# Moving matmul operands in on-chip memory: the distance from the streamed operand to the loaded one, modulo 128 words

## The reference, cut to what matters

```python
# block 1: norm, in-projection, gated-recurrence and window attention, out-projection,
#          memory cross-attention, then for each token 128 of 16384 experts:
u = expert_down[eidx]
a = gelu(einsum('thkd,td->thk', u, xb))
y = einsum('thkk,thkd->td', g * a, expert_up[eidx])       # h = h + y
...
# block 2, twice: a mixer and a feed-forward
h = h + mixer(rms_norm(h)) ; h = h + conv_ffn(rms_norm(h), w_up, w_down)
def conv_ffn(hn, w_up, conv_w, conv_b, w_down):
    u, v = split(hn @ w_up, 2)                            # 1024 -> 2 x 2816
    return (silu(depthwise_conv3(u)) * v) @ w_down        # 2816 -> 1024
```

## Time and profile before

| | |
|---|---|
| time, median of 3 runs | 1670.4 us (1668.63 to 1673.06) |
| profiled execution, first to last instruction | 1670.5 us |
| PE / PEld busy | 1652.9 / 1542.5 us |
| DVE / ACT busy | 1237.3 / 935.2 us |
| DMA | 323.40 MB, mean 194 GB/s |
| TensorE clock granted | full speed (2.4 GHz), shown as 1.00, in every stretch below (from 17 us on) |

### The profile page before, as it was taken

The page is one execution under the profiler, slowest core; times in us unless marked ns, Lnnn a source line. Parts: engine busy times, 40 slices in busy tenths (PEclk is TensorE's granted clock), DMA queues, the critical chain, the costliest instruction groups (busy, mean ns, idle before and its releaser), DMA issues.

```text
span 1670.5 us, 30280 instructions
## 1 busy us (share of the span) xinstructions
PE 1652.9 (99%) x12006; PEld 1542.5 (92%) x12006; DVE 1237.3 (74%) x1896; ACT 935.2 (56%) x1139; POOL 242.8 (15%) x333
## 2 busy tenths in 40 slices
PE   8999999999999999999999999999999999999999
PEld 8999999999999999988888888999999888899987
DVE  6875467999998666667676676887888565769974
ACT  7885565555546555545555454786545357565542
POOL 0000000004667676211010110000000000100000
PEclk9999999999999999999999999999999999999999
DMA  7445344776555555777777776533555544345553
GB/s 304 152 152 180 120 159 157 231 233 213 189 178 191 190 189 191 270 240 238 245 235 239 241 238 222 221 133 139 184 185 195 180 174 152 124 156 203 200 188 115
DMA packets 73804, 323.40 MB, mean 194 GB/s; under 512 B 8663, under 2 KB 9047, under 8 KB 55744
## 3 DMA queue, kind: packets, MB, share of 16 engines
q1 hardware_dynamic: 58736, 285.18, 50.1%
q0 software_dynamic: 5568, 19.38, 3.7%
q10 hardware_dynamic: 9360, 16.92, 2.7%
HBM read 303.62 MB, written 17.83 MB: 192 GB/s over the span
## 4 chain that ended last, share of the span: by engine, by line
PE 83%; DVE 12%; ACT 4%; issue 1%; DMA 0%; SPq 0%; ACTq 0%; DVEq 0%
PE bank L605 14%; PE bank L606 13%; PE bank L607 13%; PE bank L986 7%; PE bank L985 7%; PE bank L987 7%; PE bank L938 5%; PE bank L942 5%; PE bank L941 5%; DVE lo_u L2299 3%; PE bank L950 2%; DVE wlo L1914 2%; DVE oh L2310 1%; ACT whi L1350 1%; DVE pos L2196 1%
## 5 line engine op out<-in xcount | busy, mean ns | idle before, releaser
L1586 ACT ACTIVATE hi_u<-raw_u 128x1024 fp32r<-128x1024 f32 x256 | 271.8, 1062 | 279.6 <-PE bank L985 165.2
L1914 DVE TENSOR_TENSOR wlo<-raw,whi 128x2048 fp32r<-128x2048 f32 (+1 forms) x141 | 314.7, 2232 | 105.6 <-PE bank L605 83.3
L1350 ACT ACTIVATE whi<-raw 128x2048 fp32r<-128x2048 f32 x137 | 263.1, 1920 | 77.6 <-PE bank L605 74.7
L938 PE MATMUL bank<-xh,hi_u 128*128 128x256 f32 x1024 | 291.9, 285 | 1.5 <-DVE lo_u L2299 1.2
L2299 DVE TENSOR_TENSOR lo_u<-raw_u,hi_u 128x1024 fp32r<-128x1024 f32 x192 | 237.9, 1239 | 70.4 <-PE bank L938 62.4
L941 PE MATMUL bank<-xl,hi_u 128*128 128x256 f32 x1024 | 285.4, 279 | 0.0
L942 PE MATMUL bank<-xh,lo_u 128*128 128x256 f32 x1024 | 285.3, 279 | 0.0
L605 PE MATMUL bank<-nh,whi 128*128 128x256 f32 x904 | 253.4, 280 | 0.5 <-DVE wlo L1914 0.4
L607 PE MATMUL bank<-nh,wlo 128*128 128x256 f32 x904 | 251.9, 279 | 0.0
L606 PE MATMUL bank<-nl,whi 128*128 128x256 f32 x904 | 251.9, 279 | 0.0
L519 POOL TENSOR_SCALAR oh<-kept,sel_T 128x128 f32<-128x128 f32 x256 | 199.9, 797 | 249.3 <-ACT sel_T L1636 166.4
(11 more groups left out here) (417 smaller groups left out, 3358.7 us busy)
## 6 DMA issues: line engine op xcount, KB each, us to landing
raw<-in_weights SPq DMA_DIRECT2D x138, 1024.0 KB, 4.8
raw_u<-in_experts SPq DMA_DIRECT2D x256, 512.0 KB, 4.2
aside<-a_out ACTq DMA_DIRECT2D x64, 256.0 KB, 3.6
a_in<-aside POOLq DMA_DIRECT2D x64, 256.0 KB, 3.7
const<-in_const SPq DMA_DIRECT2D x1, 1409.0 KB, 9.0
const<-in_const POOLq DMA_DIRECT2D x1, 1409.0 KB, 6.4
h<-in_x SPq DMA_DIRECT2D x2, 512.0 KB, 5.1
raw<-in_weights SPq DMA_DIRECT2D x2, 512.0 KB, 7.6
```

The lines of the kernel that those rows point to most:

```text
L938: mm = pe.matmul(out, w[0][:, kp], xh[:, k, :], start=(k == 0), stop=False)
L1350: a(A(whi[:, n % HIGH, :], raw[:, n % RAW, :], ACT.Copy), S("weights_hi"))
L1586: a(A(hi_u[:, u % HIGH_U, :], raw_u[:, u % RAW_U, :], ACT.Copy), S("unit_high"))
L1914: v(V.tensor_tensor(wlo[:, n % LOW, place], raw[:, n % RAW, place], whi[:, n % HIGH, place].bitcast(F32), ALU.subtract), S("weights_split" ...
```

## The change

Only addresses change. On every engine the instructions and their waits are the same, in the same order; `xh` to `gl1` in the table lie elsewhere.

| stage | matmuls | distance before | after |
|---|---|---|---|
| first in-projection, `xh`/`xl` stream | 264 | 16 | 8 |
| first in-projection, `xh`/`xl` stationary | 192 | -16 | -8 |
| experts down (`xh`/`xl`) | 3072 | 16 | 8 |
| experts up (`chi`/`clo`), 512 columns | 1512 | 48 | 8 |
| even mixer (`nh4`/`nl4`) | 672 | 16 | 8 |
| feed-forward 0 up (`nh5`/`nl5`) | 1056 | 16 | 8 |
| feed-forward 0 down (`gh0`/`gl0`), 512 columns | 264 | 48 | 8 |
| odd mixer (`nh6`/`nl6`) | about 600 | 16 | 0 |
| feed-forward 1 up (`nh7`/`nl7`) | 1056 | 16 | 0 |
| feed-forward 1 down (`gh1`/`gl1`), 512 columns | 264 | 48 | 0 |
| `xmh`, `memh`, `nh1`, `chi0` and their low parts | | as they were | as they were |

`lo_up`, the third low buffer of the up half, moves from the memory of `xl` to that of `xh`, and keeps its residue; `chi`, `clo` and `g_final` move behind it.

```diff
         CROSSING_AT = keep.at
-        keep.at += 64
+        keep.at += 72
         XH = keep.at
         xh = keep("xh", KD, T, dt=F32R)
         xl = keep("xl", KD, T, dt=F32R)
-        keep.at += 64
-        mixed = Area(XH + 32)
+        keep.at = CROSSING_AT + 2 * KD * T + 128
+        mixed = Area(CROSSING_AT + 96)
...
         crossing = Area(CROSSING_AT)
+        crossing.beside(HIGH_AT, 0)
+        lo_up = crossing("lo_up", UNIT, dt=F32R)
+        crossing.beside(HIGH_AT, 8)
         chi = crossing("chi", 2, 2, T, dt=F32R)
         clo = crossing("clo", 2, 2, T, dt=F32R)
         g_final = crossing("g_final", D)
-        crossing.beside(HIGH_AT, 0)
-        lo_up = crossing("lo_up", UNIT, dt=F32R)
+        assert crossing.at <= CROSSING_AT + 2 * KD * T + 128
...
-        for n_, by in ((4, 16), (5, -16), (6, 16), (7, -16)):
+        for n_, by in ((4, 8), (5, -8), (6, 0), (7, 0)):
             block2 = Area(BLOCK2)
             block2.beside(HIGH_AT, by)
             halves_of.append((block2(f"nh{n_}", KD, T, dt=F32R), block2(f"nl{n_}", KD, T, dt=F32R)))
...
-        for layer_, by in ((0, 48), (1, 48)):
+        for layer_, by in ((0, 8), (1, 0)):
             halves = Area(ARENA2)
             halves.beside(HIGH_AT, by)
             gated_of.append((halves(f"gh{layer_}", 22, T, dt=F32R), halves(f"gl{layer_}", 22, T, dt=F32R)))
```

## The result

The changed kernel takes 1695.05 us (median of 4 runs, 1694.45 to 1696.81), the kernel before 1669.52 us (median of 4). The ratio is 1.0153, with an interval of 1.0136 to 1.0169. I had said 1652, with a range up to 1676.

The account below looks back on a forecast made before the run. PE, busy 99% of the span, was taken to bound the kernel through the pace from one matmul's start to the next. 1670.5 - 20.5 + 1.3 = 1651.3 us, stated as 1652, range 1646 to 1676.

Parts of the forecast that it names:

- what could change the time: On PE, only the pace from one matmul's start to the next can change; issue, moves, waits and clock stay.
- two levels at 16: 256-column stages at distance 16 run at 113.3 or 117.8 ns, about half each, switching only at an interruption.
- the reading of -16: First in-projection, xh stationary: 9.28 / 79 = 117.5 ns from 60 us, taken as the slow level.
- I take the fast level for 8 and 0: Stages moved to 8 or 0 run at 113.3 ns for 256 columns and 226.8 ns for 512.
- the bounds: Pace at 8 and 0 lies between 113.3 and 117.8 ns for 256 columns, 226.8 and 231.3 for 512.
- the slow rival: 8 words is inside the conflict of stream and load, everything fast becomes slow: 19.6 us more, 1690; chance 0.20.
- a way out, at 1678: Case within the slow rival: only the stages at 8 are bad and those at 0 good, 1678.
- The prediction's own sign of being wrong: Wrong if 281 ns matmuls remain in the stages at 8, or if some stage shows a third level.
- Terms of the sum: Gains forecast stage by stage from slow matmuls becoming fast and 512-column matmuls gaining 2.2 ns each, together 20.5 us.
- The 1.3 us to be given back to DVE: From 275 to 530 us, a faster PE leaves DVE less time; a quarter of 5.1 us is lost, 1.3 us.
- The rival without placement: Levels come from the restart alone and the 2.2 ns from something else; placement is worth 0, 1670; chance 0.10.
- the five terms of the prediction's sum for its 256-column stages: Gains at the fast level: experts down 7.2, even mixer 1.6, feed-forward 0 up 4.8, odd mixer 1.0, first in-projection 1.4 us.

Follow-up runs that it names:

- the two halves: Changed kernel with 256-column stages back at 16: 1676.38 us, ratio 1.0033 to the kernel before; changed kernel with 512-column stages at 0: 1684.19 us, 1.0086.

## Why the prediction was wrong, step by step

**Right: what could change the time.** Only the pace from start to start changed. PE waits as little as before, and stage lengths add up to the span.

**Right: two levels at 16, changed only at an interruption.** The same stage at the same distance was fast in one kernel and slow in another (feed-forward 0 up: 117.8 in the kernel before, 113.2 with everything shifted). Without an interruption it held: 958 steps in one piece at 117.8 in the one, as many at 113.3 in the other. No experiment shows what decides the level, or that it is chance.

**Wrong: the reading of -16.** The prediction called it "the slow level" from one stretch, 60 to 69 us. The same `chunk` matmuls, `xh` stationary at the same distance, run at 113.3 ns a few us later; by the count, 5.28 / 47 = 112.3, where one matmul more or less is 2.4 ns, and the slow level would give 45:

```profile
core 0: us, PE busy (x), PEclk, DMA share, GB/s
72.70:77.70 5.00, 5.00 (x47) 1.00 0.71 238
```

So -16, which is 48 modulo 64, had both levels before the change, as 16 had, and was no evidence that a distance can be slow throughout.

**Wrong, and the cause of the miss: "I take the fast level for 8 and 0, because the only row within 16 words, at 0, has it, and the two rows away from it (-16, 48) do not."** Two things were taken from one row. The first was that the pace is smooth in the distance, so that 8 lies between 0 and 16. It is not: under 512 columns 0 is 226.7 and 8 is 233.3, and under 256 columns 14 and 18 are 120.0 while 16 is 113.3 or 117.8. The second was that a row of 512 columns tells about 256. It does not: 0 is the best distance there and, with 40, the worst multiple of 8 here. The row itself was read rightly, as the 512-column stages at 0 show (4.8 us gained where 4.6 were worked out).

**Wrong: the bounds.** I put the slow level, 117.8 and 231.3 ns, above 8 and 0 because no row was slower. Both distances go beyond it: 118.4 and 120.0 ns, 233.3 under 512 columns. The two levels seen at one distance are no bound for another, and so even the slow rival, at 1690, fell short of 1695. Its sign was right for the stages at 8: everything that was fast there became slow. Whether a conflict of stream and load is the reason is not shown. For the stages at 0 it had the fast level as a way out, at 1678 (its own terms, 12.8 us lost at 8 and 1.6 gained at 0, give 1682), and 0 turned out to be the worse of the two under 256 columns. The prediction's own sign of being wrong, a stage at a third level, came in seven of the eight stages of the table of the result.

**Terms of the sum.** Forecast and measured change of stage length, in us: experts down -7.2 and +5.1, experts up -3.3 and +6.6, feed-forward 0 up -4.8 and +0.6, feed-forward 1 up 0 and +6.4, odd mixer -1.0 and +2.4, even mixer -1.6 and +1.1, the first in-projection -1.4 and +0.6, the two down-projections -1.2 and +0.5. Only feed-forward 1 down gained (0.4; its share of the term was 0.6). In experts down the pace alone, 2.7 ns on 3072 matmuls, would be 8.2; 3.1 of it do not show, since the interruptions between units got shorter. Why they did is open; a slower PE leaves DVE more time, and PE's wait for `lo_u` fell from 1.2 to 0.4 us, which may be a part. The 1.3 us to be given back to DVE had nothing to come from.

**The rival without placement.** The Trainium skill (SBUF — State Buffer, "SBUF: two separate sides") says that on the engine side only the shared port pair contends and that PE never waits on anyone. The prediction took from it that placement is worth nothing, the rival at 1670 with 0.10. The runs contradict that conclusion: ratios of 1.0086 and 1.0033 for the two halves, 0.997 for the 512-column stages at 0, all from addresses alone.

**Open.** The mechanism behind the pattern. Shown are: the distance between stream and load changes the pace, and a shift of everything by 8 words does not; the pattern repeats every 64 words at the four distances that have a partner; 256 and 512 columns have different best distances; changing one stage leaves the pace of the others at what their own distances give. That stream and load meet in one memory is still only an argument, supported by the widened step under which `clo` is loaded. What decides between the levels of a distance is open, and so are the different paces of 12, 14 and 18 words in different stages. Could the fast level at 16 be had always, it would be worth an estimated 16.0 us in the kernel before, the five terms of the prediction's sum for its 256-column stages.

## What to carry to other kernels

When PE is busy 99% of the time, compare the step from one matmul's start to the next between stages of the same shape. A few per cent between equal stages with equal waits was an effect of placement and of the level here, and the shown duration of a matmul has only a trace of it (276 against 281 and 283 ns). Where operands lie relative to each other is then a parameter to be measured, for each stream width separately, at every multiple of 8 words modulo 64. Read every stretch of a stage, not one: a single stretch shows one level of possibly several. One row at one distance and width says nothing of the next distance or the other width. Put different distances into the different stages of one kernel, and one profile gives seven or eight points of the sweep.

## What the runs showed of the hardware that was not expected

- float32r matmuls at full clock never stepped faster than 113.3 ns for 256 columns and 226.7 ns for 512, by the mean step of a steady stretch of 40 matmuls or more, in any of the 13 traces.
- A period of 64 words in the distance: 16 and 80, 0 and 64, 32 and 96, 48 and 112 agree within 0.3 ns (16 and 80, and 48 and 112 under 256 columns, in both of their levels).
- One of three loads at distance 8 costs 512-column matmuls as much as all three: 700 ns for three, against 680 at 0.
- Two words off 16 the up-projections lose 6.7 ns a matmul against the fast level (120.0 against 113.3).
